# Second attention of a two-block transformer kernel: a pair's scores issued ahead of a turn and a product, some exponentials ahead of a copy

## The reference

```
proj = rmsnorm(h) @ w_in                 # a_u, a_v, q, k, v, forget logits
a_out = spatial_gating(gelu(a_u), gelu(a_v))
c = cumsum(log_sigmoid(f_logit + b_f))   # per head
for head in 8, for block i of 128 queries:
    logits = q_blk @ k[: (i+1)*128].T * 64**-0.5 + c_q - c_k   # causal
    o = softmax(logits) @ v[: (i+1)*128]                       # head dim 64
mix = concat(rmsnorm(a_out), rmsnorm(o)) @ w_out
h = h + rmsnorm(mix);  h = h + rmsnorm(mlp(rmsnorm(h)))
```

## Time and profile before

| what | us |
|---|---|
| median of 3 runs | 2554.58 |
| lowest, highest | 2554.26, 2558.36 |
| the profiled execution | 2554.64 |
| its span in the profile | 2552.7 |
| PE busy in the span | 2415.6 (95%) |
| DVE, ACT, POOL busy | 1473.3, 799.4, 1154.0 |

### The profile page before, as it was taken

How to read it: one execution, slowest core, us unless ns; L and a number is a source line. 1 busy time by engine, 2 the same in 40 slices (tenths; PEclk the granted TensorE clock), 3 DMA queues, 4 the chain that set the end, 5 groups by cost and what they waited for, 6 DMA issues and landing times.

```text
span 2552.7 us, 32735 instructions
## 1 busy us (share of the span) xinstructions
PE 2415.6 (95%) x11678; PEld 1956.9 (77%) x11678; DVE 1473.3 (58%) x2113; ACT 799.4 (31%) x1517; POOL 1154.0 (45%) x888
## 2 busy tenths in 40 slices
PE   8997888897999999999999998889989999999997
PEld 7976756676788888888778886778768888888885
DVE  5974766536555655555574302664645655556556
ACT  4231356624222222222241002552532222222222
POOL 3210040353655566555582533001745665556553
PEclk8998899899999999999999998999999999999999
DMA  5445520032111111111242122001311111111114
GB/s 147 125 132 132 174 77 1 7 104 96 42 58 49 58 53 49 49 49 49 91 157 64 50 66 83 10 1 42 131 42 51 59 51 49 49 49 49 49 54 156
DMA packets 176914, 179.28 MB, mean 70 GB/s; under 512 B 39704, under 2 KB 139544, under 8 KB 176816
## 3 DMA queue, kind: packets, MB, share of 16 engines
q1 hardware_dynamic: 171520, 164.02, 21.2%
q10 hardware_dynamic: 5296, 13.96, 1.6%
HBM read 147.46 MB, written 30.49 MB: 70 GB/s over the span
## 4 chain that ended last, share of the span: by engine, by line
PE 83%; DVE 8%; ACT 3%; issue 2%; POOL 2%; DMA 2%; ACTq 0%; SPq 0%; POOLq 0%; DVEq 0%
PE ps L267 23%; PE ps L269 23%; PE ps L268 23%; PE ps L1466 3%; PE ps L1498 3%; PE ps L1484 2%; PE ps L474 1%; DVE hbuf L425 1%; ACT ex L1546 1%; DVE hbuf L2013 1%; PE ps L2737 1%; DVE ex L1577 0%; PE ps L456 0%; DMA msb<-ssm_lags 0%; DVE hbuf L431 0%
## 5 line engine op out<-in xcount | busy, mean ns | idle before, releaser
L2013 DVE TENSOR_TENSOR hbuf<-hbuf,ps 128x1024 f32<-128x1024 f32 x320 | 390.7, 1221 | 245.5 <-PE ps L269 223.7
L267 PE MATMUL ps<-mlp_dh,mlp_fh 128*128 128x512 f32 x672 | 263.8, 393 | 4.9 <-DVE hbuf L2013 4.4
L269 PE MATMUL ps<-mlp_dh,mlp_fl 128*128 128x512 f32 x672 | 263.0, 391 | 0.0
L268 PE MATMUL ps<-mlp_dl,mlp_fh 128*128 128x512 f32 x672 | 262.2, 390 | 0.0
L207 POOL TENSOR_TENSOR wgt<-raw,ones 128x512 fp32r<-128x512 f32 x76 | 87.2, 1147 | 322.6 <-PE ps L269 165.5
L1779 POOL TENSOR_TENSOR mlp_s_raw<-mlp_gh_raw,mlp_s_raw 128x512 f32<-128x512 f32 x44 | 57.2, 1299 | 284.1 <-PE ps L269 284.1
L267 PEld LDWEIGHTS ps<-mlp_dh,mlp_fh 128*128 128x128 f32 x672 | 126.3, 188 | 35.7 <-DVE hbuf L2013 8.2
L269 PEld LDWEIGHTS ps<-mlp_dh,mlp_fl 128*128 128x128 f32 x672 | 126.3, 188 | 27.5
L268 PEld LDWEIGHTS ps<-mlp_dl,mlp_fh 128*128 128x128 f32 x672 | 126.4, 188 | 27.3
L1792 POOL TENSOR_TENSOR mlp_dl<-mlp_d_raw,mlp_dh 128x1024 fp32r<-128x1024 f32 x42 | 114.0, 2713 | 46.5 <-ACT mlp_dh L1991 46.5
L2050 DVE TENSOR_TENSOR mlp_fl<-mlp_p,mlp_fh 128x512 fp32r<-128x512 f32 x42 | 114.4, 2725 | 3.6
(11 more groups left out here) (483 smaller groups left out, 6696.8 us busy)
## 6 DMA issues: line engine op xcount, KB each, us to landing
h<-hbuf SPq DMA_DIRECT2D x24, 512.0 KB, 2.9
mlp_d_raw<-in_w_down SPq DMA_DIRECT2D x21, 512.0 KB, 3.5
mlp_d_raw<-in_w_ffn_out SPq DMA_DIRECT2D x21, 512.0 KB, 3.7
raw<-in_w_in SPq DMA_DIRECT2D x40, 256.0 KB, 2.8
raw<-in_w_out SPq DMA_DIRECT2D x32, 256.0 KB, 2.8
res_b<-h SPq DMA_DIRECT2D x16, 512.0 KB, 4.4
mlp_ul<-in_w_up SPq DMA_DIRECT2D x22, 256.0 KB, 3.0
mlp_uh_raw<-in_w_up SPq DMA_DIRECT2D x22, 256.0 KB, 3.3
```

Of the source, the lines that this page charges most:

```text
L267: pe.matmul(out, lhs[0], rhs[0], start=first, stop=False, skip_group_check=over)
L268: pe.matmul(out, lhs[0], rhs[1], start=False, stop=False, skip_group_check=over)
L269: return pe.matmul(out, lhs[1], rhs[0], start=False, stop=last, skip_group_check=over)
L2013: v.tensor_tensor(self.acc[:, i, :], self.acc[:, i, :], src, ALU.add).then_inc(self.s["added"], 1)
```

## The change

Three of its parts touch the second attention; the first is built as before.

- On TensorE the scores of pair (n+3, n+4), n odd, stand in iteration n ahead of the turn of item n+1's first batch and of the last product of item n. Before they stood behind both, at the head of iteration n+1. Those of the 256 pair of the first group stand ahead of the first turn.
- On ScalarE the exponential of item n+2 stands ahead of the copy of item n+1's first batch, where ScalarE has that copy.
- On VectorE the output of item n is written at the head of iteration n+1 in place of the end of iteration n.

```diff
         def three_ahead(self, n):
+            if self.maps == 1:
+                return n % 2 == 1 and n + 3 < len(self.items)
             return n + 3 < len(self.items) and not self.wide(n + 3)
@@ pe
             if self.maps == 2:
                 self.pe_scores(pe, 1)
-                self.pe_scores(pe, 2)
+            self.pe_scores(pe, 2)
             self.pe_turn(pe, 0)
             for n in range(len(self.items)):
-                if n + 2 < len(self.items) and (self.wide(n + 2) if self.maps == 2 else n % 2 == 0):
+                if self.maps == 2 and n + 2 < len(self.items) and self.wide(n + 2):
                     self.pe_scores(pe, n + 2)
                 for b in range(self.first[n], self.first[n + 1]):
-                    if self.maps == 2 and b + 1 == self.first[n + 1] and self.three_ahead(n):
+                    if b + 1 == self.first[n + 1] and self.three_ahead(n):
                         self.pe_scores(pe, n + 3)
@@ act
-                    if self.maps == 2 and b == self.first[n + 1] and n + 2 < len(self.items):
+                    if b == self.first[n + 1] and n + 2 < len(self.items):
                         self.act_exp(act, n + 2)
...
-                if self.maps == 1 and n + 2 < len(self.items):
-                    self.act_exp(act, n + 2)
@@ dve
-                if self.maps == 2 and n >= 1:
+                if n >= 1:
                     self.dve_out(v, n - 1, link)
...
-                if self.maps == 1 or n == N - 1:
+                if n == N - 1:
                     self.dve_out(v, n, link)
```

## The result

| | before | changed |
|---|---|---|
| median, us | 2554.98 (2554.26 to 2558.36, 4 runs) | 2584.87 (2579.73 to 2590.66, 4 runs) |
| ratio to before | | 1.0113, 95% interval 1.0092 to 1.0134 |
| the profiled execution, us | 2554.64 | 2590.66 |

The changed kernel is 1.1% slower, 29.9 us by the medians. Its profiled execution is the slowest of its four runs, 5.8 us above the median, so what the trace shows in all is somewhat more than the median lost. Each ratio in this document is against runs of the kernel before that were taken beside it (medians 2553.63 to 2556.93 us), and one of e7's twelve runs, 3022.8 us at a mean granted clock of 0.743 where the others have 0.97 to 0.98, is in its median but not in its ratio.

What follows compares the result with a forecast made beforehand. It took TensorE, busy but for 20.1 us of waits in the second attention, as the bound. Group terms 11.8 + 5.0 + 0.75 + 3.0 made 20.6 us, 2575; with clock falls it predicted 2578, range 2566 to 2590.

Steps and rivals of the forecast that it cites:

- (4): Second attention: the summed waits plus a clock fall in one or two narrow steps a group, 2578 to 2583 us; 40%.
- (5): Second attention: clock low for most narrow steps, four in each of three groups, 14 us more, 2590 us; 10%.
- The moved scores wait for maxima: TensorE's moved scores wait for VectorE's negated maximum, some seven times a group, 1.6 to 1.8 us narrow, 0.4 to 0.9 wide.
- The rival of gain: Second attention: earlier scores bring earlier exponentials and the waits go; 2534.5 us for all, 2544.5 for half; 4%.
- (2): Second attention: both orders cost the same, the maximum's wait merely replacing the exponential's; 2552 to 2559 us; 6%.
- (6): Wide steps: part of their price hidden as first turns find copies earlier, 6 us less, 2569 us; 5%.
- The step formula: One pair's scores to the next: scores, turn, copy, outputs, two maxima and semaphore summed; 384 to 512 gives 4.08 against 3.54.
- the term w: VectorE's semaphore as seen by TensorE at the end of a step, taken as 0.15 us.
- The sum: Longer steps over four groups of the second attention: 20.6 us in all, within 15 to 24 if the clock holds.
- The first group: First group of the second attention: 384 scores start 1.6 us earlier, yet the group costs 3.0 us more in all.
- The clock: Narrow steps of three groups: granted clock falls in one or two each, 1.0 to 1.3 us a step, 3 to 8 us.
- The rule on bubbles: Gaps ahead of TensorE's turns: a consistent bubble can mean too little SBUF or PSUM, so earlier scores could not profit.

Runs made afterwards that it cites:

- e7: Against the kernel before: scores of only the 256 to 640 pairs moved, with VectorE's list putting their maxima ahead of copies and scalings; 2551.08 us, ratio 0.9986.
- e6: Changed kernel with VectorE's output scaling really moved behind the next first maximum, the inverse staying ahead of it; 2567.81 us, ratio 1.0054.
- e1: Changed kernel with ScalarE's exponentials put back behind the copies, so only the scores are moved; 2584.8 us, ratio 1.0116.
- e2: Against the kernel before: only ScalarE's sixteen exponentials moved ahead of a copy, scores not moved; 2554.93 us, ratio 0.9996.
- e5: Changed kernel plus two unread matmul calls on TensorE ahead of the scores of the 384 to 768 pairs; 2574.66 us, ratio 1.0082.
- e3: Changed kernel with only the scores of the 256 to 768 pairs moved, the others placed as before; 2573.47 us, ratio 1.0066.

## Why the prediction was nearly right, and where it was off

The prediction was 2578 us and slower; the median is 2584.87, inside its range. It lies between the prediction's (4), one or two falls of the clock a group, and (5), a clock low for most narrow steps.

- *VectorE's part is no change: price 0.* Right. Its list is the same, and the timeline above has the output ahead of the maximum as before. e6 shows what a move that deserves the name is worth on the moved scores.
- *ScalarE's part: price 0.* Right, by e1 and e2.
- *The moved scores wait for maxima that have a copy and an output ahead of them.* Right. The profile has what was named for it: 28 waits, seven in a group, one wait for an exponential left, and a first maximum 1.2 us after its scores (1 to 1.5 foretold). What was foretold as the length of such a wait, 1.6 to 1.8 in narrow steps, is 1.61 in one narrow step and 1.38 to 1.42 in three, with about 0.2 beside it for a copy; in wide steps it is 0.28 to 0.55 (0.4 to 0.9 foretold). The rival of gain is out: it needed the second maximum ahead of the moved scores. So are those that hid the wide steps' price, (2) and (6), by steps of 7.20 and 7.54 at full clock where before had 6.21 and 6.76.
- *The step formula.* Where the clock is 1.00 each step can be laid beside its sum: 3.97 against 4.08, 4.70 against 4.81, 5.43 (e5) against 5.54, 6.85 against 6.85, 7.20 against 7.27, 7.54 against 7.61. Most of them are about 0.1 short, and that is the term w. I took it from a copy, 0.15. Behind the short last instruction of a maximum it is 1627.96 - 1627.91 = 0.05. Only 128 to 256 is longer than its sum, 5.60 against 5.54. The group is 45.07 against 45.6.
- *The sum.* What e5 costs in the medians, 21.0 us, stands against the sum of 20.6, but so near a match is partly luck. In the traces the stage, from its first scores to the first matmul behind it (L2204, in e5 L2209), takes 1732.23 - 1564.27 = 167.96 before and 1750.75 - 1563.58 = 187.17 in e5. That is 19.2 us, and it includes the 1.4 that a filler adds in the first group. Each whole group is 0.5 below its sum; the end, from the last 1024 scores on, is 1.2 longer than before where 0.75 was taken.
- *The first group.* It begins better, as foretold: from the stage's first scores to the 384 scores it takes 1573.35 - 1566.39 = 6.96, against 1572.81 - 1564.27 = 8.54 before, 1.6 earlier. The whole group is 48.23 against 42.51, with the clock low in most of it up to the 768 scores. In e5 it is 45.17, 2.7 longer, where 3.0 were foretold; with the filler's 1.4 in it and a clock that rises sooner, that is no check of the terms.
- *The clock: 3 to 8 us.* This is the term that was mis-sized. I let it fall in one or two narrow steps of three groups, at 1.0 to 1.3 each. By e5 it is 8.9 to 10.2 in the median. In the profiled execution, the slowest, the stage takes 1768.26 - 1566.39 = 201.87, 14.7 more than in e5, the size of (5). Three things were wrong in the term. Each group has two to four steps hit, not one or two, and from group to group they cost 3.1, 3.1, 3.6 and, in the last up to its 1024 scores, 4.9 us against e5. A hit costs more than 1.0 to 1.3 in the longer steps: in the second group 640 to 768 is 6.94 against e5's 5.43 and 768 to 896, beyond the narrow steps, 8.48 against 6.85; in the third group 512 to 640 is 5.84 against 4.70, and 640 to 768 is 7.92 against 5.43, 2.5 longer and the dearest of all. Its rows:

```profile
1682.01 2.51 PE L1466 MATMUL ps<-k,q 64*128 64x512 f32 x8 [1.24 <-DVE negmax L1588]
...
1689.93 1.56 PE L1466 MATMUL ps<-k,q 64*128 64x512 f32 x8 [1.38 <-DVE negmax L1588]
```

And the falls come in all four groups, not in three.
- *The rule on bubbles.* The Trainium skill, Perfetto Trace Analysis, Identifying Performance Opportunities, names too little PSUM as a cause of a gap that comes again and again. The trace agrees in part: the scores, issued earlier, waited 27.3 us for their banks. But with the same four banks they wait 22.5 us in e3 (five narrow pairs moved) and 1.7 us in e7 (four, with VectorE's list to match), so how long the banks are held depends on the order of that list.

What stays open: the exact share of the clock. The intervals of the changed kernel and of e5 are each about 5 us to either side, and the falls differ from trace to trace: the second group takes 48.20 in the changed kernel and 46.90 in e1, with the same lists on TensorE and VectorE. Nor did I run a kernel in which the scores have banks of their own, which would test the banks as the cause directly.

## What to carry to other kernels

Before moving a producer's instruction ahead of others, look in the consumer's list at what stands ahead of its consumer: if that waits for the very instructions just passed over, the move can be worse than none. Move both lists or neither; here either alone, in the narrow steps, cost 0.6 to 0.7%, and both together cost nothing (0.9986), and gained 0.5% when the copies that were late next went to another engine. Of a new short wait on TensorE count its length and also what it may do to the clock in the wider steps behind it.

## What the runs showed of the hardware

- With waits of at most 1.6 us, one a step, and a shorter one beside it, the granted clock fell from 1.00 to about 0.6 in the mean of 4 us; ahead of the fall TensorE was busy for 2.41 and 3.23 us of 4. Matmuls that nobody reads, in those waits, held it at 1.00 from the second group on and made the kernel 8.9 to 10.2 us faster.
- Against e5's steps at full clock a fall cost 1.1 to 1.4 us at 512 to 640, 1.5 to 2.5 at 640 to 768 and 1.5 to 1.6 at 768 to 896.
- VectorE's end seen by TensorE: 0.05 us behind the one-column negated maximum, against 0.15 behind the copy of 512 columns; one pair of rows each.
